# Seven block products for 12 chunks of each first feed-forward, with vector work reordered and the conditioning moved

## What is computed

```python
def half_ffn(x, g, w1, w3, w2):
    return x + 0.5 * swiglu(rmsnorm(x, g), w1, w3, w2)      # w1, w3: 1024 x 2816, w2: 2816 x 1024
def swiglu(h, w1, w3, w2):
    return (silu(h @ w1) * (h @ w3)) @ w2
# second model: 6 * 1024 numbers in each of two layers, used in both mixers and feed-forwards
mod = silu(c) @ w_ada[l] + b_ada[l]
```

## Time and profile before

| | us |
|---|---|
| median of 3 runs | 3132.42 |
| lowest, highest | 3131.48, 3132.74 |
| the profiled execution | 3134.22 |
| its span, first to last instruction | 3132.4 |

### The profile page before, as it was taken

How to read it: one execution, slowest core, us unless ns; L and a number is a source line. 1 busy time by engine, 2 the same in 40 slices (tenths; PEclk the granted TensorE clock), 3 DMA queues, 4 the chain that set the end, 5 groups by cost and what they waited for, 6 DMA issues and landing times.

```text
span 3132.4 us, 39304 instructions
## 1 busy us (share of the span) xinstructions
PE 3120.2 (100%) x15840; PEld 2629.8 (84%) x15840; DVE 2040.7 (65%) x3069; ACT 1274.8 (41%) x1908; POOL 156.5 (5%) x170
## 2 busy tenths in 40 slices
PE   9999999999999999999999999999999999999999
PEld 7888878888888888888888888887898988789898
DVE  5457567445755456647644575888893868889574
ACT  5322264322234222264332223556452545745342
POOL 2000000000000000000000000113000002400000
PEclk9999999999999999999999999999999999999999
DMA  5345422334542335422233454221223233022322
GB/s 151 94 134 180 136 85 88 101 94 135 189 141 82 104 125 168 155 94 82 81 100 102 135 181 146 69 81 39 83 95 118 86 103 97 15 94 94 109 92 84
DMA packets 334348, 340.00 MB, mean 109 GB/s; under 512 B 12503, under 2 KB 329209, under 8 KB 334169
## 3 DMA queue, kind: packets, MB, share of 16 engines
q1 hardware_dynamic: 332144, 333.80, 33.4%
q0 software_dynamic: 1792, 3.62, 0.4%
q10 hardware_dynamic: 232, 0.06, 0.0%
HBM read 335.36 MB, written 2.10 MB: 108 GB/s over the span
## 4 chain that ended last, share of the span: by engine, by line
PE 92%; DVE 4%; ACT 3%; DMA 0%; issue 0%; SPq 0%; DVEq 0%
PE ps L138 90%; PE ps L141 2%; ACT ar L95 1%; DVE wl L100 1%; DVE ar L108 1%; DVE ar L100 1%; ACT wh L95 0%; DVE hl L108 0%; DMA raw<-in_ffn_w 0%; DVE T L108 0%; ACT L95 0%; ACT sp L95 0%; ACT T L95 0%; DVE ar L123 0%; DVE ar L111 0%
## 5 line engine op out<-in xcount | busy, mean ns | idle before, releaser
L100 DVE TENSOR_TENSOR wl<-raw,wh 128x1024 fp32r<-128x1024 f32 (+3 forms) x709 | 728.4, 1030 | 421.0 <-ACT wh L95 418.9
L138 PE MATMUL ps<-hh,wl 128*128 128x512 f32 (+1 forms) x2632 | 991.7, 377 | 2.0 <-DVE wl L100 1.1
L138 PE MATMUL ps<-hh,wh 128*128 128x512 f32 (+1 forms) x2632 | 984.7, 374 | 0.0
L138 PE MATMUL ps<-hl,wh 128*128 128x512 f32 (+1 forms) x2632 | 984.3, 374 | 0.0
L95 ACT ACTIVATE wh<-raw 128x1024 fp32r<-128x1024 f32 (+3 forms) x709 | 628.4, 896 | 536.2 <-PE ps L138 458.7
L138 PE MATMUL ps<-ul,wh 128*128 128x512 f32 (+1 forms) x1664 | 585.4, 356 | 0.0
L138 PEld LDWEIGHTS ps<-hh,wl 128*128 128x128 f32 x2632 | 496.0, 188 | 95.9 <-issue 8.2
L138 PEld LDWEIGHTS ps<-hh,wh 128*128 128x128 f32 x2632 | 496.0, 188 | 88.9
L138 PEld LDWEIGHTS ps<-hl,wh 128*128 128x128 f32 x2632 | 496.3, 189 | 85.6 <-issue 0.2
L138 PE MATMUL ps<-uh,wl 128*128 128x512 f32 (+1 forms) x1568 | 557.3, 355 | 0.8 <-ACT sq L95 0.8
L138 PE MATMUL ps<-uh,wh 128*128 128x512 f32 (+1 forms) x1568 | 555.9, 354 | 0.0
(11 more groups left out here) (258 smaller groups left out, 2898.6 us busy)
## 6 DMA issues: line engine op xcount, KB each, us to landing
raw<-in_ffn_w SPq DMA_DIRECT2D x119, 1024.0 KB, 5.3
raw<-in_w_ada SPq DMA_DIRECT2D x48, 1024.0 KB, 5.2
raw<-in_w_gate_up SPq DMA_DIRECT2D x44, 1024.0 KB, 5.1
raw<-in_m_w_in SPq DMA_DIRECT2D x26, 1024.0 KB, 5.4
raw<-in_w_down SPq DMA_DIRECT2D x16, 1024.0 KB, 5.2
raw<-in_ffn_w SPq DMA_DIRECT2D x16, 768.0 KB, 4.9
raw<-in_w_in SPq DMA_DIRECT2D x12, 1024.0 KB, 5.4
raw<-in_m_w_out SPq DMA_DIRECT2D x8, 1024.0 KB, 5.2
```

Source lines behind the costliest of these rows:

```text
L100: return self.issue(lambda e: e.tensor_tensor(out, a, b, op))
L138: return self.issue(lambda e: e.matmul(out, l, r, start=start, stop=stop, skip_group_check=True))
```

## The change

- WOVEN gets 12 chunks of each first feed-forward: w3 of j = 2, w1 of j = 3 to 10, w3 of j = 4, 6 and 8. The last ones keep their 17. With that the first feed-forwards have two output parts too.
- ADA_AFTER puts all conditioning chunks into first output parts: ten in each first feed-forward (one behind each odd tile of each of the two w2 chunks, two behind tile 3 of the first and tile 5 of the second), eight in the first of the last ones. Readers of layer 0 wait for chunk 23 in place of 47.
- The lists of the two splitting engines are sorted by a due number, `before` + 1; for products 6 and 5 it is one and two later (at most two products ahead of their use). The mixes are entries of VectorE's list with due numbers of their own.
- The four sums of `differences` run at the start of a first feed-forward. The product of a woven tile with R and the gate product, so far directly behind the join, and the low part come one or two steps later (`settle`, `gated`).
- POOL issues the loads for the gate stages behind the start of the final output part.

```diff
@@ -167,10 +167,11 @@
 FFNS = (("ffn", 0, 0), ("ffn", 0, 1), ("ffn", 1, 0), ("ffn", 1, 1), ("ffn2", 0), ("ffn2", 1))
-WOVEN = {s: ({("w3", 2), *((w, j) for j in range(3, 11) for w in ("w1", "w3"))} - {("w3", 10)}) if s[0] == "ffn2" else set() for s in FFNS}
+WOVEN = {s: {("w3", 2), *((w, j) for j in range(3, 11) for w in ("w1", "w3") if w == "w1" or s[0] == "ffn2" or j % 2 == 0)} - {("w3", 10)} for s in FFNS}
 PARTS = (1, 4, 6, 5)
-ADA_AFTER = ({("post", "w3", 2 * j + 1) for j in range(7, 11)} | {("out", (k0, kt), 2 * m + 1) for m in range(3) for k0, kt in ((0, 8), (8, 8), (16, 6)) if m < 2 or k0 < 16},
-             {("post", "w3", 15), ("post", "w3", 19), *(("out", k, t) for k in ((0, 8), (8, 6)) for t in (1, 3, 5, 7)), ("out", (14, 8), 1), ("out", (14, 8), 3)})
+ADA_AFTER = {s: {("out", k, t): 1 + (s[0] == "ffn" and (k, t) in (((0, 8), 3), ((8, 6), 5))) for k in ((0, 8), (8, 6)) for t in (1, 3, 5, 7)}
+             for s in FFNS[:5]}
+ADA_AFTER[FFNS[5]] = {}
 SHARE = {1: (0, 0), 5: (0, 0), 3: (0, 0), 2: (1, 0), 4: (1, 1), 6: (1, 1), 7: (0, 1)}
@@ -346,9 +347,10 @@
                 ada_at.append(n_mm[0])
-                ada_due[max(n_mm[0] + 1, 5)] = i
-        def plan_ffn(key, w1, w3, w2, with_ada):
+                if i % 8 == 7:
+                    ada_due[max(n_mm[0] + 1, 5)] = i
+        def plan_ffn(key, w1, w3, w2):
             at = {}
@@ -369,12 +371,11 @@
                     n_mm[0] += 1
-                if with_ada and (what, w, i) in ADA_AFTER[bool(WOVEN[key])]:
-                    plan_ada(1)
+                plan_ada(ADA_AFTER[key].get((what, w, i), 0))
...
             if st[0] == "ffn":
-                plan_ffn(st, I['ffn_w1'][st[1], st[2]], I['ffn_w3'][st[1], st[2]], I['ffn_w2'][st[1], st[2]], True)
+                plan_ffn(st, I['ffn_w1'][st[1], st[2]], I['ffn_w3'][st[1], st[2]], I['ffn_w2'][st[1], st[2]])
             elif st[0] == "mix0":
@@ -412,7 +413,7 @@
                 W = I['w_gate_up_2'][l]
-                plan_ffn(st, W[:, 0:NF], W[:, NF:2 * NF], I['w_down_2'][l], False)
+                plan_ffn(st, W[:, 0:NF], W[:, NF:2 * NF], I['w_down_2'][l])
         assert len(ada_at) == 48
@@ -432,6 +433,30 @@
             halves[0] += some
+        due = {g: before[g] + 1 for g in before}
+        for g, (s, w, j, p) in part_of.items():
+            if p in (6, 5):
+                due[g] = min(due[g] + (1 if p == 6 else 2), g - 2)
+        hi_order = sorted(due, key=lambda g: (due[g], g))
+        lo_order, last = [], 0
+        for o in order:
+            if o[0] == "ada":
+                lo_order.append((max(due[last], 2), last, 1, o))
+            else:
+                last = o[1]
+                lo_order.append((due[last], last, 0, o))
+        for g, (s, w, j, p) in part_of.items():
+            at_part = {c: due[G_of[(s, w, j, "part", c)]] for c in (1, 3, 4, 5)}
+            if p == 1:
+                lo_order.append((due[g], g, 1, ("mix", 7, part_of[g], shape[g][0])))
+            elif p == 4:
+                lo_order.append((due[g] + 1, -3, 0, ("mix", 6, part_of[g], shape[g][0])))
+                lo_order.append((due[g] + 1, -1, 0, ("mix", 5, part_of[g], shape[g][0])))
+            elif p == 3:
+                late = at_part[3] - 2 <= at_part[5]
+                lo_order.append((max(at_part[3] - 2, at_part[5]), g if late else -2, 1, ("mix", 3, part_of[g], shape[g][0])))
+        lo_order.sort(key=lambda c: c[:3])
@@ -1501,14 +1526,13 @@
             act = Scalar(e)
-            mms = [o for o in order if o[0] == "mm"]
             at = [0]
...
-                while at[0] < len(mms) and before[at[0]] < g:
-                    i = at[0]
+                while at[0] < len(hi_order) and due[hi_order[at[0]]] <= g:
+                    i = hi_order[at[0]]
                     at[0] += 1
@@ -1684,7 +1708,7 @@
             def differences(s):
-                for _ in range(3 if s == STAGES[0] else 4):
+                for _ in range(1 if s[0] == "ffn" else 4):
                     yield 1
@@ -2347,7 +2371,7 @@
                     if k == 0:
-                        dve.wait_ge(*left_of(("ada", 47)))
+                        dve.wait_ge(*left_of(("ada", 47 if s[1] else 23)))
                         if s[0] == "ffn2":
@@ -2373,22 +2397,20 @@
-            def mixed_weights(s, w, j, p, n):
-                def mix(dst, a, b, op):
-                    dve.tt(quarter_of(n, dst), quarter_of(n, a), quarter_of(n, b), op).then_inc(worked, (s, w, j, dst, "weights"))
-                if p == 1:
-                    mix(7, 1, 7, SUB)
-                elif p == 4:
+            def mixed_weights(dst, chunk, n):
+                s, w, j, _ = chunk
+                a, b, op = {7: (1, 7, SUB), 6: (4, 7, SUB), 5: (6, 1, ADD), 3: (2, 6, SUB)}[dst]
+                if dst == 6:
                     dve.wait_ge(worked, (s, w, j, 7, "weights"))
                     dve.wait_ge(lo_split, G_of[(s, w, j, "part", 4)])
-                    mix(6, 4, 7, SUB)
-                    dve.own()
-                    mix(5, 6, 1, ADD)
-                elif p == 7:
+                elif dst == 5:
+                    dve.wait_ge(worked, (s, w, j, 6, "weights"))
+                    dve.wait_ge(lo_split, G_of[(s, w, j, "part", 1)])
+                elif dst == 3:
+                    dve.wait_ge(worked, (s, w, j, 6, "weights"))
                     dve.wait_ge(lo_split, G_of[(s, w, j, "part", 5)])
-                    mix(3, 2, 6, SUB)
+                dve.tt(quarter_of(n, dst), quarter_of(n, a), quarter_of(n, b), op).then_inc(worked, (s, w, j, dst, "weights"))
@@ -2401,17 +2423,15 @@
                         o.then_inc(*((worked, ("mod", i, q)) if q < 3 else (left(("ada", i)), ("ada", i))))
-                while at[0] < len(order):
-                    o = order[at[0]]
-                    if (before[o[1]] >= g) if o[0] == "mm" else (g < 2):
-                        return
+                while at[0] < len(lo_order) and lo_order[at[0]][0] <= g:
+                    o = lo_order[at[0]][3]
                     at[0] += 1
...
                         dve.tt(lo, src, hi.bitcast(F32), SUB).then_inc(lo_split, o[1])
-                        if o[1] in part_of:
-                            mixed_weights(*part_of[o[1]], o[2])
+                    elif o[0] == "mix":
+                        mixed_weights(*o[1:])
                     else:
@@ -2491,7 +2511,7 @@
                 l = s[1]
-                dve.wait_ge(*left_of(("ada", 47)))
+                dve.wait_ge(*left_of(("ada", 47 if l else 23)))
                 return dve.stt(G[:, :], mod[:, 48 * l + 8 * sc:48 * l + 8 * sc + 8], 1.0, cols(name, 8 * l, 8), ADD, MUL)
@@ -2641,16 +2661,20 @@
                     dve.tt(to, y[:, :], sq[woven_at[s, w, j] % 2][:, :], ADD).then_inc(left((s, "Y", w, j)), (s, "Y", w, j))
-                if s[0] == "ffn" and w == "w1":
-                    dve.own()
+            def gated(s, w, t):
+                to = (T1 if w == "w1" else T3)[t % 2][:, :]
+                done = (worked, (s, "odd", w, t // 2)) if t % 2 else left_of((s, "Y", w, t // 2))
+                dve.wait_ge(*done)
+                if w == "w1":
                     dve.tt(to, to, R[:, :], MUL).then_inc(worked, (s, "gate", t))
-                if w == "w3":
-                    dve.own()
+                else:
                     silu_done(s, t)
-                    dve.tt(to, to, T1[a][:, :], MUL).then_inc(worked, (s, "gv", t))
+                    dve.tt(to, to, T1[t % 2][:, :], MUL).then_inc(worked, (s, "gv", t))
...
             def differences(s):
-                if s != STAGES[0]:
+                if s[0] == "ffn2":
                     yield 1
@@ -2709,8 +2733,24 @@
                 if WOVEN[s]:
-                    dve.beside(differences(s))
+                    token = dve.beside(differences(s))
+                    if s[0] == "ffn":
+                        next(token)
+                        next(token)
                 chain, later = None, []
+                def settle():
+                    for c in list(later):
+                        c[0] -= 1
+                        if c[0] == 0:
+                            later.remove(c)
+                            if c[1] == "low":
+                                low_gated(s, c[2])
+                            else:
+                                gated(s, *c[1:])
+                                if c[1] == "w3":
+                                    later.append([2, "low", c[2]])
                 for what, w, i, p in rounds(s):
@@ -2718,14 +2758,13 @@
                     if what in ("part", "post"):
-                        while later:
-                            low_gated(s, later.pop(0))
+                        settle()
                     if what == "post":
...
                         joined(s, w, i, p)
-                        if w == "w3":
-                            later.append(2 * i + p)
+                        if w == "w3" or s[0] == "ffn":
```

(8 more changed lines are left out.)

## The result

The changed kernel is slower: 3189.09 us against 3132.38 us, a ratio of 1.0179 with the 95% interval 1.0159 to 1.0199. One of its four executions took 7930.17 us, at full clock and for no reason that is known; it is left out of the ratio (the other three have their median at 3188.06 us). The profiled execution took 3188.06 us with a span of 3185.7. The forecast was 3097.5 us.

What follows compares the result with a forecast made beforehand. It took TensorE alone to bound the first feed-forwards, as long as VectorE keeps up. 3134.2 us less 37.9 saved plus 3.0 for entries and bursts gave 3099.3, median 3097.5 us; own range 3093 to 3102.

Steps and rivals of the forecast that it cites:

- TensorE's saving: First feed-forwards: each of 48 chunks falls from 10.87 to 10.08 us as seven products, 37.9 us less in all.
- VectorE's forecast of 78%: Whole span: VectorE busy near 78% after the change, 2041 us before and 95 us more per feed-forward.
- the section on the seven-product chunks: VectorE in woven chunks: a pair needs 20.1 us in 20.16 us of TensorE, so it costs almost nothing.
- The last feed-forwards gain or lose nothing by these edits: Last feed-forwards: no change beyond the first one's 8 conditioning chunks, 34 us in a 76 us part.
- The new due numbers: Woven-chunk entries: splits of products 6 and 5 come later, so ScalarE's partial sum copy is no longer behind them.
- Entries and bursts: 24 entries into woven chunks of first feed-forwards: between 0 and 13.7 us, taken as 3 us with all bursts.
- The first output part: VectorE there needs 71.6 us against 76.1 of TensorE; 0 to 3.5 us lost per part, taken as nothing.
- The clock: TensorE, whole kernel: read as nearly always at its full clock; the sum has no term for a slower one.
- (a): Rival: VectorE's in-order queue makes gaps, 0.57 us at 24 entries, 3108 us, or 3122 with output parts; chance 22%.
- (b): Rival: VectorE bounds the first output part, 19.6 us per feed-forward, 3173 us; decides from 9.5 us each; chance 6%.
- (c): Rival: seven products don't bring TensorE below the plain pace beside this VectorE load, 3132 us; chance 3%.
- (d): Rival: TensorE's weight loads stand beside no matmul, 120 us slower, 3252 us; chance 1%.

Runs made afterwards that it cites:

- e1: Changed kernel with the gate product and the product with R directly behind the join again, low part one step later: 3111.59 us, ratio 0.9936.
- e8: e1 with 17 instead of 12 woven (seven-product) chunks in each first feed-forward: 3100.01 us, ratio 0.9897.
- e6: Changed kernel with only the gate product of woven w3 tiles back behind the join, low part one step later: 3126.28 us, ratio 0.9981.
- e5: Changed kernel, late products kept, with ScalarE's conversion and silu one product later too and a wait ahead of the first partial sum's copy: 3163.21 us.
- e4: Changed kernel with conditioning chunks out of the first output pair, never two in a row, some behind w3 and w1 tiles: 3215.79 us, ratio 1.0269.
- e11: Changed kernel with no conditioning chunk in or ahead of the first output pair, but later in that part and in the final part: 3195.19 us.
- e10: Kernel before with the late products alone; woven chunks, split order and conditioning places as before: 3151.68 us, ratio 1.0062.
- e12: Kernel before with the new order of splits and mixes alone, products at once: 3130.50 us, ratio 0.9995.
- e3: Changed kernel with the order of splits and mixes, the gate product and the product with R as before: 3132.30 us, ratio 1.0002.
- e7: e1 with the doubled conditioning chunks taken apart, two moved behind tiles 1 and 3 of the final output part: 3111.60 us, ratio 0.9934.

## Why the prediction was wrong

**What bounds the kernel, and TensorE's saving: right.** 17568 matmuls came, and e1 and e8 show the saving in the time. e1's feed-forward (0,1) is 4.6 us shorter than before. In the earlier trace rows weight loads and matmuls are both busy for the whole 50 us of a seven-product stretch, so they overlap, though the matmuls there use all 128 rows; the rule of the Trainium skill (TensorE: Matmul & The Clock Gate, Part 3, The mechanism) is not borne out here. VectorE's forecast of 78% came out at 75% of a longer span, 2390 us for 2423.

**The step that failed** is in the section on the seven-product chunks. It counts VectorE's operations per pair, finds them just fitting, and costs every movement within VectorE's program at nothing or as a gain. The late gate product and the late product with R stand in the change's description, and the sum has no term for them. What was put at nothing measured 77 us (changed kernel against e1), 63 with the gate product and its low part and 15 with the product with R (e6). Three ways are shown. The reader of the moved product stands in its own queue with other work behind it: ScalarE's conversion, with a partial sum's copy behind. Moving it along gave back 26 us (e5). And the moved low part comes to stand behind conditioning work: five waits of 4.89 us and the slow clock behind them, gone where the conditioning chunk is elsewhere (e4, e11) or the product comes at once (e1). The late product with R, last, makes the silu late, the plain w3 product behind it and so the next splits: part of the waits for wl, which fall from 23.3 to 10.2 us in e1.

**"The last feed-forwards gain or lose nothing by these edits"** is the same mistake where it could have been seen most easily: they lost 24 us. e10, with the old order of splits, loses 20 us there with no operation added.

**The new due numbers: right in kind, too small in size.** They do lift the wait of the earlier trace rows (e12), worth 1.6 us or nothing that can be told in the kernel before (the interval holds 1), but 20.7 us with woven chunks in the first feed-forwards (e3 against e1). Without them 12 woven chunks would have gained nothing at all.

**Entries and bursts: 3 us, mis-sized.** With the products at once 3111.6 is left against the forecast of 3097.5: 17 us lost in place of 3, 2.4 to 4.9 us in each first feed-forward; 10.2 us in the whole kernel are waits for wl. The rest is open: feed-forward (1,0) of e1 is 2.4 us short, and only 1.2 us of that are waits for wl.

**The first output part:** I took nothing, from a bound of 0 to 3.5 us. The 5 us gap, with 2 us of slow clock behind it, was outside the bound, because the bound was VectorE's sum and the gap is one low part behind 4.3 us of conditioning work. In e1, where the low part is not behind it, this part has no such gap; two waits of 1.11 and 0.81 us for wl are left in the four first output parts. That is within the bound of 3.5 us.

**The clock:** the sum had it at full speed throughout. It mostly is. The waits of 4.89 us here and of 3.1 us and more in e11 each brought a stretch at half clock. But one stands in the kernel before as well, with no wait ahead of it; TensorE had done 16 matmuls of one column in 1.9 us just before:

```profile
174.00:176.00 2.00, 2.00 (x6) 1.59 (x5) 1.05 (x3) 1.58 (x2) 0.00 (x0) 0.50 0.00 0
```

**The rivals.** (a) named the kind, gaps by VectorE's in-order queue, but priced it at 0.57 us per entry and placed it where the load is full; the gaps came where the load had fallen to 85%. (b) gave the right sign by the wrong mechanism, a full VectorE, and was excluded by e1 and e8. The point from which it decides was passed all the same: some 17 us per feed-forward against 9.5. So its sign came true by luck. (c) and (d) are excluded by e1, at 3111.6 us; the 120 us of (d) would be 126 by its own figures.

**Open:** which of the remaining waits for wl in e1 and e8 come from the differences at the start of a feed-forward; no run takes these apart.

## What to carry to other kernels

When a change moves an operation later in one engine's program, list who reads its result, what stands behind that reader in the reader's own queue, and move the reader too; a load sum per engine says nothing about it. Put long work without a deadline (here conditioning, 4.3 us) where nothing that is due sooner than its length stands behind it. And look at the stages that a change should not touch: a difference there is the change's order, not its load.

## What the runs showed of the hardware

After a stop of 4.89 us TensorE ran ten matmuls of 512 columns at 0.43 us, a granted clock of 0.52, before it was back at 0.226 us. After one of 3.25 us in e11 the clock was 0.50 over the next 5 us and 0.86 over the 5 after. The waits of 1.3 to 1.5 us in the seven-product stretches left it at 1.00, and so did one of 2.32 us in e11. The same stop of 3.12 us at the start of feed-forward (0,0) was followed by half clock in e1 (0.66 over 5 us) and not in e6 and e7 (1.00). VectorE fed TensorE without loss of pace at up to 98% of its time (e8, 640 to 660 us), more than I had dared to assume.
